# A two-layer trunk kernel: the down projection leaves the feed-forward units and becomes a stage of seven block products

## The reference, cut to what matters

```python
h = rms_norm(x, norm2_g[l]) * (1.0 + sc2) + sh2
x = x + g2 * ((jax.nn.silu(h @ w_gate[l]) * (h @ w_up[l])) @ w_down[l])
```

## Time and profile before

| | |
|---|---|
| median of 3 runs | 2955.24 us (2953.01 to 2957.68) |
| span of the profiled execution | 2955.1 us |
| PE busy | 2893.3 us (98%), 14180 matmuls |
| DVE, ACT, POOL busy | 2089.2, 1148.2, 1141.8 us |
| feed-forward stage of layer 0 and of layer 1 | about 840 to 1492 us and 2288 to 2939 us of the span |

### The profile page before, as it was taken

How to read it: one execution, slowest core, us unless ns; L and a number is a source line. 1 busy time by engine, 2 the same in 40 slices (tenths; PEclk the granted TensorE clock), 3 DMA queues, 4 the chain that set the end, 5 groups by cost and what they waited for, 6 DMA issues and landing times.

```text
span 2955.1 us, 40205 instructions
## 1 busy us (share of the span) xinstructions
PE 2893.3 (98%) x14180; PEld 2441.5 (83%) x14180; DVE 2089.2 (71%) x2601; ACT 1148.2 (39%) x1825; POOL 1141.8 (39%) x783
## 2 busy tenths in 40 slices
PE   6999999999999999999989999999999999999998
PEld 6888889988878888888878888898887788888887
DVE  7899688854686666666668896887535776666766
ACT  3433377751242222222342335777224322222223
POOL 0355322332644444444425452233323534343443
PEclk9999999999999999999999999999999999999999
DMA  7565400125511111111145552001341111111111
GB/s 287 165 194 185 139 9 16 51 71 194 185 33 54 50 56 47 56 50 57 33 151 164 185 172 70 17 26 38 123 157 54 46 51 53 54 49 55 49 57 68
DMA packets 279184, 263.66 MB, mean 89 GB/s; under 512 B 46737, under 2 KB 237329, under 8 KB 277650
## 3 DMA queue, kind: packets, MB, share of 16 engines
q1 hardware_dynamic: 252464, 217.66, 24.0%
q10 hardware_dynamic: 26594, 44.32, 4.1%
HBM read 218.59 MB, written 40.96 MB: 88 GB/s over the span
## 4 chain that ended last, share of the span: by engine, by line
PE 90%; DVE 4%; ACT 2%; POOL 2%; issue 1%; DMA 1%; SPq 0%; POOLq 0%; DVEq 0%; ACTq 0%
PE ps L679 16%; PE ps L681 16%; PE ps L682 16%; PE ps L1714 9%; PE ps L1716 9%; PE ps L1715 9%; PE ps L1574 3%; PE ps L1594 2%; PE ps L1595 2%; PE ps L1555 2%; PE ps L1560 2%; PE ps L1559 2%; POOL e_lo L1289 1%; POOL sq_sum L1117 1%; DMA ada_rows<-in_w_ada 1%
## 5 line engine op out<-in xcount | busy, mean ns | idle before, releaser
L626 POOL TENSOR_TENSOR wlo<-blocks,whi 128x512 fp32r<-128x512 f32 x368 | 504.1, 1374 | 729.4 <-ACT whi L620 729.4
L3011 DVE SCALAR_TENSOR_TENSOR x_sb<-ps,mod,x_sb 128x1024 f32<-128x1024 f32 x320 | 404.5, 1280 | 244.8 <-PE ps L682 237.1
L620 ACT ACTIVATE whi<-blocks 128x512 fp32r<-128x512 f32 x368 | 228.0, 629 | 761.5 <-PE ps L1716 671.0
L663 POOL TENSOR_TENSOR wlo<-raw,whi 128x1024 fp32r<-128x1024 f32 (+4 forms) x156 | 235.9, 1529 | 709.6 <-ACT whi L655 709.4
L679 PE MATMUL ps<-h_hi,whi 128*128 128x512 f32 x832 | 282.1, 402 | 12.7 <-DVE h_lo L2568 7.6
L681 PE MATMUL ps<-h_lo,whi 128*128 128x512 f32 x832 | 275.5, 394 | 0.0
L682 PE MATMUL ps<-h_hi,wlo 128*128 128x512 f32 x832 | 274.4, 392 | 0.0
L1714 PE MATMUL ps<-h_hi,whi 128*128 128x512 f32 x640 | 250.6, 391 | 3.9 <-POOL wlo L626 3.9
L1715 PE MATMUL ps<-h_lo,whi 128*128 128x512 f32 x640 | 250.2, 391 | 0.0
L1716 PE MATMUL ps<-h_hi,wlo 128*128 128x512 f32 x640 | 250.2, 391 | 0.0
L655 ACT ACTIVATE whi<-raw 128x1024 fp32r<-128x1024 f32 (+4 forms) x162 | 106.9, 699 | 347.9 <-PE ps L682 291.5
(11 more groups left out here) (347 smaller groups left out, 6715.3 us busy)
## 6 DMA issues: line engine op xcount, KB each, us to landing
ada_raw<-in_w_ada SPq DMA_DIRECT2D x64, 512.0 KB, 4.5
raw<-in_w_in SPq DMA_DIRECT2D x92, 256.0 KB, 4.8
blocks<-in_w_down SPq DMA_DIRECT2D x88, 256.0 KB, 2.7
blocks<-in_w_gate SPq DMA_DIRECT2D x84, 256.0 KB, 2.8
blocks<-in_w_up SPq DMA_DIRECT2D x84, 256.0 KB, 2.9
gate_scratch<-gst ACTq DMA_DIRECT2D x32, 512.0 KB, 4.5
gl<-gate_scratch SPq DMA_DIRECT2D x32, 512.0 KB, 4.0
ada_rows<-in_w_ada SPq DMA_DIRECT2D x16, 512.0 KB, 5.8
```

The lines of the kernel that those rows point to most:

```text
L620: act.activation(block_view(whi, s), blocks[:, r, :], ACT.Copy).then_inc(block_hi.sem, 1)
L626: pool.tensor_tensor(block_view(wlo, s), blocks[:, r, :], block_view(whi, s).bitcast(F32), ALU.subtract)\
L663: last = pool.tensor_tensor(dst(wlo[:, s, :]), src(raw[:, s, :]), dst(whi[:, s, :].bitcast(F32)), ALU.subtract)
L3011: dve.scalar_tensor_tensor(x_sb[:, d, :], pair(banks + 2 * (d % 2)), mod[:, 5, d:d + 1], x_sb[:, d, :], ALU.mult, ALU.add).then_inc(dn_ev. ...
```

## The change

The down projection is taken out of the units. After unit 21 comes a stage of its own (`down_step`). Here, too, a 2 x 2 block form with seven products is used: the blocks are pairs of hidden tiles (11 pairs, `DPAIRS`), the two halves of the 1024 output features, and the two halves of the tokens. Product P1 runs over all 11 pairs, then P6, P2, P7, P5, P4, P3: 77 steps (`DSTEPS`), each of 4 output tiles by 3 matmuls, 12 in all. A product accumulates in four PSUM banks; at the end of a product DVE (once ACT) takes the banks out (`down_evictions`).

- A unit keeps its seven block products and loses 48 matmuls, two weight blocks, the splitting of the hidden tile, and eight additions to x. The block products come in another order, and `e3`'s low parts go from POOL to DVE.
- The gated hidden tiles stay float32. DVE forms their sums (`hidden_sums`, 4 for a pair) and SP stores seven blocks for a pair in DRAM (`hidden_away`). Likewise DVE forms four sums of the down weights for a pair (`weight_pair_sums`, in units 2, 3, 5, 7, 8, 10, 12, 13, 15, 17, 19), from a load of 1 MB, and SP stores 1 MB.
- In the down stage each step loads one weight block and one hidden block (256 KB each; four buffers); ACT makes both high parts, POOL the weight's low part and DVE the hidden's (three buffers). A step's splitting may begin when the step three before it is done on PE.
- The squares for the next norm, its first steps, and the loads and splits of the next layer's first weights are placed beside steps of the down stage. The loops are written out.

```diff
-    BLOCKS = ("A11", "S1", "A12", "DN0", "S3", "A22", "S2", "S4", "DN1")
-    PLAIN_BLOCKS = ("A11", "A21", "A12", "A22", "DN0", "DN1")
-    LAST_BLOCKS = ("A11", "S1", "A12", "S3", "A22", "S2", "DN0", "DN1", "S4", "DN0_END", "DN1_END")
-    W_SLOT = {"A11": 0, "S3": 0, "S1": 1, "A22": 1, "A12": 2, "S2": 2, "S4": 2, "DN0": 3, "DN1": 3}
-    PLAIN_SLOT = {"A11": 0, "A12": 1, "A21": 2, "A22": 3, "DN0": 0, "DN1": 2}
-    TAIL_PLACE = {"DN0": 0, "DN1": 1, "DN0_END": 2, "DN1_END": 3}
-    TAIL_BANK = ((0, 1, 2, 3, 4, 5, 0, 1), (2, 3, 4, 7, 0, 1, 2, 3))
-    RAW_SLOT = {"A11": 0, "A12": 1, "A21": 2, "S3": 2, "A22": 3, "S1": 4, "S2": 5, "S4": 5, "DN0": 6, "DN1": 7,
-                "DN0_END": 6, "DN1_END": 0}
+    PLAIN_BLOCKS = ("A11", "A21", "A12", "A22")
+    BLOCKS = ("A11", "S1", "S3", "S2", "A12", "A22", "S4")
+    W_SLOT = {"A11": 0, "S1": 1, "S3": 2, "S2": 3, "A12": 0, "A22": 1, "S4": 2}
+    PLAIN_SLOT = {"A11": 0, "A12": 1, "A21": 2, "A22": 3}
+    RAW_SLOT = {"A11": 0, "A12": 1, "A21": 2, "S3": 2, "A22": 3, "S1": 4, "S2": 5, "S4": 5}
     SUMS = ("S1", "S3", "S2", "S4")
+    DPAIRS = FT // 2
+    W_PAIR_UNIT = tuple(2 + 17 * j // 10 for j in range(DPAIRS))
+    DOWN = ("P1", "P6", "P2", "P7", "P5", "P4", "P3")
+    DSTEPS = 7 * DPAIRS
+    D_WEIGHT = {"P1": "A11", "P6": "S2", "P2": "A12", "P7": "S3", "P5": "S1", "P4": "A22", "P3": "S4"}
+    D_HIDDEN = {"P1": 0, "P5": 1, "P2": 2, "P3": 3, "P4": 4, "P7": 5, "P6": 6}
+    SUM_PLACE = {"S2": 0, "S3": 1, "S4": 2, "S1": 3}
+    D_BANK = {"P1": 0, "P2": 0, "P5": 0, "P3": 0, "P6": 4, "P7": 4, "P4": 4}
+    D_OPENS = ("P1", "P6", "P7", "P5")
+    DVE_LOWS = (70, 71, 72)
...
-                def down_tiles(f, i, banks, tiles):
-                    side = (f - 1) % 2
-                    for d in tiles:
-                        if d == 0:
-                            pe.wait_ge(hid_ready.sem, hid_ready.at(l, 2 * f) + 4 * i)
-                        if d % 4 == 0:
-                            block_ready(f, "DN1" if d else "DN0", i)
-                        s = block_slot(f, "DN1" if d >= 4 else "DN0")
-                        if d >= 2:
-                            pe.wait_ge(dn_ev.sem, dn_ev.at(l, KT * (f - 1) + d - 1) + 2 * KT * i)
-                        b = banks + 2 * (d % 2)
-                        end = products(pe, [ps[:, b, :], ps[:, b + 1, :]], block_view(whi, s, d % 4),
-                                       block_view(wlo, s, d % 4),
-                                       [(hid_hi[side][:, half_cols(t)], hid_lo[side][:, half_cols(t)]) for t in range(2)],
-                                       True, True)
-                        end[1].then_inc((slot_used[s] if d % 4 == 3 else dn_mm).sem, 1)
...
+                def down_step(n):
+                    p, j = divmod(n, DPAIRS)
+                    name = DOWN[p]
+                    if j == 0:
+                        if name == "P1":
+                            wait(pe, hid_mul, l, 2 * LAST)
+                        elif name == "P6":
+                            wait(pe, hid_mul, l, 2 * FT)
+                        elif name == "P2":
+                            pe.wait_ge(u_copied.sem, u_copied.at(l, 4))
+                        else:
+                            pe.wait_ge(d_ev.sem, d_ev.at(l, {"P7": 4, "P5": 16, "P4": 20, "P3": 28}[name]))
+                    d_weight_ready(pe, l, n)
+                    pe.wait_ge(d_lo_h.sem, d_lo_h.at(l, n + 1))
+                    for m in range(4):
+                        col = slice(m * P, (m + 1) * P)
+                        end = products(pe, [ps[:, D_BANK[name] + m, :]], d_tile(n, 0, 0)[:, col], d_tile(n, 0, 1)[:, col],
+                                       [(d_tile(n, 1, 0), d_tile(n, 1, 1))], j == 0 and name in D_OPENS, j == DPAIRS - 1,
+                                       name not in D_OPENS)[0]
+                    end.then_inc(d_used.sem, 1)
...
+                for f in range(2, FT):
+                    ffn_unit(f)
+                for n in range(DSTEPS):
+                    down_step(n)
+                    if n == 69:
+                        mean_squares(l + 1, 0)
+                    if n == 70:
+                        norm_scale(l + 1, 0)
...
+                def hidden_away(f):
+                    j = f // 2
+                    wait(sp, hid_mul, l, 2 * f + 2)
+                    if f % 2 == 0:
+                        sp.dma_start(hidden_dram[j, :, 0, :], hid_even[:, 0, :]).then_inc(hid_stored[0].sem, 16)
+                        sp.wait_ge(hid_sum.sem, hid_sum.at(l, 4 * j + 1))
+                        sp.dma_start(hidden_dram[j, :, 1, :], hid_even[:, 3, :]).then_inc(hid_stored[1].sem, 16)
+                    else:
+                        sp.dma_start(hidden_dram[j, :, 2:4, :], hid_odd[:, :, :]).then_inc(hid_stored[2].sem, 16)
+                        sp.wait_ge(hid_sum.sem, hid_sum.at(l, 4 * j + 4))
+                        sp.dma_start(hidden_dram[j, :, 4:7, :], hid_even[:, 0:3, :]).then_inc(hid_stored[3].sem, 16)
+                def sums_away(j):
+                    sp.wait_ge(w_pair_sum.sem, w_pair_sum.at(l, 4 * j + 4))
+                    sp.dma_start(sums_dram[j], w_pair[:, :, :]).then_inc(w_pair_stored.sem, 16)
...
+                load_w_pair(0)
+                hidden_away(0)
+                for f in range(2, LAST):
+                    for name in ("A11", "A21", "A12", "A22"):
+                        slot_freed(f, name)
+                        load_block(name, f + 1)
+                    hidden_away(f - 1)
+                    if f in W_PAIR_UNIT:
+                        sums_away(W_PAIR_UNIT.index(f))
+                    if f + 1 in W_PAIR_UNIT:
+                        load_w_pair(W_PAIR_UNIT.index(f + 1))
+                for n in range(DSTEPS):
+                    if n == 2:
+                        hidden_away(LAST - 1)
+                    if n == 4:
+                        hidden_away(LAST)
+                    load_down_weight(n)
+                    load_down_hidden(n)
...
+                def weight_pair_sums(j):
+                    a11, a21, a12, a22 = (w_pair[:, n, :] for n in range(4))
+                    dve.wait_ge(w_pair_loaded.sem, w_pair_loaded.at(l, 16 * (j + 1)))
+                    dve.tensor_tensor(a22, a21, a22, ALU.add).then_inc(w_pair_sum.sem, 1)
+                    dve.tensor_tensor(a21, a11, a21, ALU.subtract).then_inc(w_pair_sum.sem, 1)
+                    dve.wait_ge(w_pair_sum.sem, w_pair_sum.at(l, 4 * j + 1))
+                    dve.tensor_tensor(a11, a22, a11, ALU.subtract).then_inc(w_pair_sum.sem, 1)
+                    dve.wait_ge(w_pair_sum.sem, w_pair_sum.at(l, 4 * j + 3))
+                    dve.tensor_tensor(a12, a12, a11, ALU.subtract).then_inc(w_pair_sum.sem, 1)
...
+                def down_evictions(n):
+                    if 23 <= n < 27:
+                        m = n - 23
+                        product_end(2)
+                        dve.wait_ge(u_copied.sem, u_copied.at(l, m + 1))
+                        dve.tensor_tensor(u_part[:, m, :], u_part[:, m, :], ps[:, 4 + m, :], ALU.add).then_inc(d_ev.sem, 1)
+                    elif 27 <= n < 31:
+                        m = n - 27
+                        evicted(m + 1)
+                        add_part(m, m, 1, u_part[:, m, :]).then_inc(d_ev.sem, 1)
+                        add_part(m, 4 + m, 0, u_part[:, m, :]).then_inc(d_ev.sem, 1)
+                    elif 34 <= n < 38:
+                        m = n - 34
+                        product_end(3)
+                        add_part(m, m, 0, ps[:, m, :]).then_inc(d_ev.sem, 1)
```

1100 lines of the change are left out of this document (532 added, 568 removed).

## The result

The changed kernel takes 2913.32 us (median of 4 runs, 2911.75 to 2918.24), the kernel before beside it 2954.12 (2948.15 to 2957.68): ratio 0.9866, 95% interval 0.985 to 0.9881. A second set on another occasion gave 2911.18 us and 0.9857 (0.9842 to 0.9872). The prediction said 2902 with 2889 to 2922: the sign, the mechanism and the range hold, and the gain is 41 us (44 from span to span) where 53 were predicted. In the text TensorE, VectorE, ScalarE, GpSimd and the sync queue are PE, DVE, ACT, POOL and SP of the rows.

A forecast was written before the change was run, and what follows sets the result against it. The prediction took PE's matmul pace, 0.2265 us each, to bound the kernel. Its terms, -59.8 + 2.4 + 10.8 + 4.0 - 7.4 - 3.3 = -53.3 us, took 2955.1 to 2902 us, range 2889 to 2922 (8 in 10).

The forecast's parts named there:

- term 1: Units and down stage: 132 fewer matmuls in a layer, 264 in all, at 0.2265 us each, -59.8 us.
- Term 2: Units 8, 10 and 12: DVE's sums reach A22 0.4 us late, in both layers, +2.4 us.
- Rival B: All units with weight sums: DVE late before A22, 29 us instead of 2.4, 2929 us in all; chance 0.12.
- Term 3: Entry to unit 2: waits before A11, S1, S3 and A22 plus lost clock, 9.7 us instead of 4.3, +10.8 us.
- Term 4: Start of the down stage: step 4's loads late behind two stores on SP, 2.0 us twice, +4.0 us.
- The steps of the stage: Down stage: other engines and transfers keep up with PE's 2.72 us a step, so 0 us added.
- Rival C: Down stage bound by its transfers at 4.0 us a step, +197 us, 3099 us in all; chance 0.05.
- Term 5, layer 0: End of layer 0: norm waits go, -3.0, and next layer's half 1 starts sooner, -4.4; -7.4 us.
- Term 5, end of the program: End of layer 1: norm waits go, -3.0, and 0.3 less behind the last matmul, -3.3 us.
- A: Whole kernel: the sum of the terms holds, 2892 to 2916 us by the bounds; chance 0.76.
- D: Larger gain: entry to unit 2 no worse than before and step 4 not late, 2887 us; chance 0.05.
- E: No change: upper-bound entry and stage-start losses, late DVE and no end-of-layer gain use up the gain; chance 0.02.

The follow-up runs named there:

- experiment 4: Changed kernel with one matmul more in each of the 154 down-stage steps (output no longer the reference's): 2938.33 us, ratio 0.9953.
- experiment 5: Changed kernel with fewer matmuls in each down-stage step, output lacking those terms: 2826.95 us with eight instead of twelve, 2821.61 us with four.
- experiment 7: Changed kernel with four more VectorE additions, result thrown away, in each of ten units with weight sums, both layers: 2958.85 us, ratio 1.0014.
- experiment 2: Changed kernel with GpSimd making S3's low part ahead of the four low parts of h at the entry to unit 2: 2918.24 us, ratio 0.9885.
- experiment 3: Changed kernel, entry to unit 2: h low parts on VectorE, first hidden store ahead of weight-pair load, first weight sums behind block sums: 2899.06 us, ratio 0.9817.
- experiment 1: Changed kernel with the last unit's two stores issued ahead of the loads of step 8 instead of step 4: 2898.87 us, ratio 0.9817.
- experiment 6: Kernel with four matmuls a down-stage step, both low parts also cut to 8 of 512 columns, output lacking low terms: 2755.07 us, ratio 0.9331.
- experiment 8: Changed kernel with 11 useless 128x512 matmuls between the last squares' small matmuls at the end of the program: 2909.95 us, ratio 0.9847.

## Why the prediction was right, and where it was off

- **What bounds the kernel, and term 1: right.** PE's pitch of 0.2265 us holds in units and stage, and 13924 matmuls were counted for "about 13920". Experiments 4 and 5 add the limit of such a term: it is worth its price only where PE doesn't wait.
- **Term 2: 0 for 2.4, and well laid out.** The hand layout put units 8, 10 and 12 0.4 us late; they came in time with nothing to spare, and the other units had 1.0 us (experiment 7). Rival B (2929) would have needed the other units 2.3 us later than they were.
- **Term 3: right, 9.2 for 10.8.** All three places came as predicted, and their releasers too, A22's by the timeline of DVE and not by the page's row; the waits were shorter before A11 (1.2 for 1.9), and the 0.3 before S1 was absent. Experiments 2 and 3 show what the sum hid: the gaps are one chain that ends before A22, and mending the largest alone costs time.
- **Term 4: the mis-sized term, 14.0 for 4.0.** The mechanism, step 4 behind two stores in the sync queue, is shown by experiment 1. The working failed at three points. The second store came 6.7 us into the stage (hidden sums until 1257.3, stage from 1250.6) and not 4.7: two low parts took VectorE 3.08 us and the first hidden sum 1.69, both beside POOL's low parts. The data came at 12.3 for 10.5, and the low part ended at 15.0 for 12.9. And the half clock behind the wait, 2.7 to 2.9 us a layer, was priced in term 3 and forgotten here. Even the upper bound of 5 us a layer was below the 7 measured. That the sum stayed inside the range is in this respect luck: its width came from other terms. The sign said that ACT or POOL would end this gap; the row names DVE's low part, behind the same DMA.
- **The steps of the stage: 0, right**, with less cover than I said. I had 1.70 us for a pair of low parts and saw the transfers as the danger; experiments 5 and 6 put the mean pace of the next bound at 2.2 to 2.4 us a step, low parts first and transfers behind. Rival C (slower) needed 3.07 us a step at 171 GB/s; the transfers made 349 with 256 KB loads. The Trainium skill (DMA: Bandwidth & Descriptors, "Bandwidth") asks for 1 MB and more in a DMA and lists 341 GB/s at that size; with several loads in flight the trace of experiment 6 reached as much with 256 KB. For a pair of low parts 1.70 us was right: experiment 5 has five in a row at that pace. The Trainium skill's exclusive lock between VectorE and GpSimd (SBUF — State Buffer, "SBUF: two separate sides"), by which a pair would cost 1.96 us, an estimate from the single durations, asks for 0.26 more than that trace shows.
- **Term 5, layer 0: right in sum, by luck in part.** -7.3 for -7.4, but the row at 1511.40 in the earlier trace rows isn't the start of half 1, as I read it: 36 matmuls lie before it and not 48. Half 1 started 22.9 us behind the last down matmul before, and 17.0 after. Against that stands the wait at step 76, which I had not looked for.
- **Term 5, end of the program: -1.2 for -3.3.** I had "no last square waiting for PE"; but there are 32 one-column passes now for 24, and the clock fell while they ran: 5.46 us for 2.86. At full clock they take 3.78 (experiment 8), so 0.9 us are the eight passes more, which the prediction had missed, and 1.7 the clock, which fell at another time in other runs of the same end.

The chances: A held, the sum with terms 2, 4 and the end of the program off; B, C, D and E did not come.

## What to carry to other kernels

A queue that issues in order is a list of due times: put a store that waits for a late result behind every load whose slot is already free (here two stores moved by four steps are worth 13 us). When several gaps follow each other, find the chain that ends last before mending one; mending the largest alone cost 5 to 7 us. Give a longer wait of TensorE a price for the half clock behind it, and give it a range: in the traces before and after 50 to 80% on top in most places, and nothing behind some waits of the same length. Price a removed instruction only up to the next engine's margin, which a deliberate extra load measures in one run, unit by unit.

## What the runs showed of the hardware that was not expected

- Loads of 256 KB, several in flight, moved 349 GB/s at a share of 0.99.
- Behind waits of 2.1 to 4.2 us TensorE mostly went on at half clock and lost 1.7 to 2.9 us more, but not always: behind the wait of 2.3 us before A22 in layer 1 of the changed kernel and behind that of 3.4 us in layer 1 of experiment 4 it kept the full clock, and so it did behind the waits of 1.2 and 1.3 us in the kernel with the entry mended.
- 32 one-column passes took 3.78 us at full clock, 5.46 when it fell 1.7 us into them and 6.59 when it fell 0.4 us into them. Filling matmuls kept the clock up beside them, but two at 0.28 us behind each group cost what they save.
- A pair of low parts on VectorE and GpSimd, back to back, passed once per 1.70 us with the transfers at a share of 0.84 beside them; over a whole stage with its other work the steps came once per 2.2 to 2.4 us.
